# Differential attention's queries and keys projected feature by token, their rotation fed by DMA block exchanges

## The reference, cut to what matters

```python
def project(h):
    q, k, v, z = jnp.split(h @ w_in, 4, axis=-1)          # each 1024 wide: 8 heads x 2 x 64
    return (q.reshape(B, L, H, 2, d) * scale, k.reshape(B, L, H, 2, d),
            v.reshape(B, L, H, 2 * d), z)
def apply_axial_rope(t, cos, sin):                        # 64 features = 2 axes x 2 halves x 16
    tf = t.reshape(t.shape[:-1] + (2, 2, quarter))
    t1, t2 = tf[..., 0, :], tf[..., 1, :]
    return stack([t1 * c - t2 * s, t2 * c + t1 * s], axis=-2).reshape(t.shape)
q_l = apply_axial_rope(q_l, cos, sin)
k_l = apply_axial_rope(k_l, cos, sin)
k_all, v_all = concatenate([k_c, k_l], 1), concatenate([v_c, v_l], 1)
```

## Time and profile before

| | |
|---|---|
| median of 3 runs | 2618.03 us (2617.14 to 2624.84) |
| profiled execution, its own time | 2614.49 us |
| its span in the trace | 2612.7 us |
| stage of the change, first matmul to last result | 1573.37 to 2028.5 us of the span |
| TensorE busy | 89% of the span |

### The profile page before, as it was taken

How to read it: one execution, slowest core, us unless ns; L and a number is a source line. 1 busy time by engine, 2 the same in 40 slices (tenths; PEclk the granted TensorE clock), 3 DMA queues, 4 the chain that set the end, 5 groups by cost and what they waited for, 6 DMA issues and landing times. The chain is left out here.

```text
span 2612.7 us, 31980 instructions
## 1 busy us (share of the span) xinstructions
PE 2334.5 (89%) x12468; PEld 1926.5 (74%) x12468; DVE 1148.3 (44%) x2048; ACT 968.7 (37%) x1876; POOL 871.8 (33%) x713
## 2 busy tenths in 40 slices
PE   5999476998999999999999968998999699999596
PEld 4899334886888888888888847787788588888265
DVE  4455365771522222222225354544110588888233
ACT  5434343781512112211224242211121477777330
POOL 3432152453323122312231142111120477777330
PEclk8999677999999999999999989999999899999798
DMA  4265733632112011201111004333441535432411
GB/s 130 79 165 138 221 119 76 180 81 81 45 53 65 29 48 54 65 25 49 57 56 50 17 17 129 109 105 105 129 143 53 161 89 131 124 99 76 166 44 73
DMA packets 223511, 237.27 MB, mean 91 GB/s; under 512 B 63576, under 2 KB 158312, under 8 KB 223360
## 3 DMA queue, kind: packets, MB, share of 16 engines
q1 hardware_dynamic: 155520, 195.36, 25.7%
q10 hardware_dynamic: 67840, 39.86, 5.5%
HBM read 170.06 MB, written 65.10 MB: 90 GB/s over the span
## 5 line engine op out<-in xcount | busy, mean ns | idle before, releaser
L1860 POOL TENSOR_TENSOR rm_w_lo<-rm_stage,rm_w_hi 128x512 fp32r<-128x512 f32 x160 | 204.8, 1296 | 553.0 <-ACT rm_w_hi L1887 552.5
L1887 ACT ACTIVATE rm_w_hi<-rm_stage 128x512 fp32r<-128x512 f32 x160 | 97.6, 625 | 286.4 <-PE rm_down L326 233.2
L326 PE MATMUL rm_down<-rm_w_hi,rm_h_hi 128*128 128x512 f32 x512 | 203.1, 397 | 0.0
L2574 DVE TENSOR_REDUCE da_low_score<-da_scores 128x1 f32<-128x1280 f32 x128 | 190.2, 1487 | 28.8 <-PE da_scores L2456 28.7
L326 PE MATMUL rm_down<-rm_w_lo,rm_h_hi 128*128 128x512 f32 x512 | 202.5, 395 | 0.0
L326 PE MATMUL rm_down<-rm_w_hi,rm_h_lo 128*128 128x512 f32 x512 | 202.4, 395 | 0.0
L308 POOL TENSOR_TENSOR dp_w_lo<-dp_stage,dp_w_hi 128x512 fp32r<-128x512 f32 x64 | 82.2, 1288 | 333.4 <-ACT dp_w_hi L297 333.3
L2557 POOL TENSOR_TENSOR da_prob<-da_prob 128x1280 f32<-128x1280 f32 x64 | 188.4, 2943 | 5.3
L2015 DVE TENSOR_TENSOR residual<-residual,rm_down 128x512 f32<-128x512 f32 x128 | 87.5, 687 | 224.2 <-PE rm_down L326 223.6
L2456 PE MATMUL da_scores<-da_k_hi,da_q 128*128 128x512 f32 (+1 forms) x384 | 151.3, 394 | 30.7 <-DMA da_k_lo<-dk_lo 26.8
L2515 ACT ACTIVATE da_prob<-da_scores,da_low_score 128x1280 f32<-128x1280 f32 x128 | 170.3, 1331 | 7.4 <-DVE da_low_score L2574 7.3
(11 more groups left out here) (378 smaller groups left out, 6488.7 us busy)
## 6 DMA issues: line engine op xcount, KB each, us to landing
rm_stage<-in_w_mlp_up SPq DMA_DIRECT2D x64, 256.0 KB, 2.9
rm_stage<-in_w_mlp_down SPq DMA_DIRECT2D x64, 256.0 KB, 3.0
dp_stage<-in_da_w_in SPq DMA_DIRECT2D x64, 256.0 KB, 3.2
gla_ada_w<-in_ada_w SPq DMA_DIRECT2D x12, 1024.0 KB, 5.2
da_k_hi<-dk_hi SPq DMA_DIRECT2D x32, 320.0 KB, 9.7
da_k_lo<-dk_lo SPq DMA_DIRECT2D x32, 320.0 KB, 11.2
dq<-dp_out_hi ACTq DMA_DIRECT2D x32, 256.0 KB, 3.7
da_q<-dq SPq DMA_DIRECT2D x16, 512.0 KB, 8.4
```

What stands on the lines that cost most here:

```text
L326: last = nc.tensor.matmul(out, x, y, start=(n == 0), stop=(n == total - 1))
L1860: nc.gpsimd.tensor_tensor(lo, stage[:, n % SLOTS], hi.bitcast(F32), ALU.subtract).then_inc(w_lo_ready, 1)
L1887: nc.scalar.activation(hi, stage[:, n % SLOTS], ACT.Copy).then_inc(w_hi_ready, 1)
L2574: nc.vector.tensor_reduce(out=low_score[:, n, z:z + 1], in_=scores[z][:, 0:K], op=ALU.min, axis=AX.X).then_inc(low_score_ready, 1)
```

## The change

Queries and keys are now made feature by token, as z was: the weights are the stationary operand, the tokens the moving one. An output is (group, kind, f, half): 128 features x 512 tokens, and for K also one of 256 context columns for each f. There are 16 Q, 16 + 8 K, 20 V and 16 Z outputs, 76 in all; 32 of them ("rope" outputs) are rotated. Eight banks hold products and no bank is kept for transposes.

For the rotation ScalarE copies the product to `x`; SP issues 8 DMAs that exchange neighbouring blocks of 16 partitions into `swapped` (SBUF to SBUF); VectorE multiplies the product by a cosine table, the exchanged copy by a signed sine table, and adds. The tables (128 x 512 each) now depend on the token half and are reloaded when the half changes (4 times after the first). ScalarE and VectorE then make high and low part. All loads and stores are issued by SP in one written order; `out_hi` and `out_lo` have two buffers each. Attention loads the query by two DMAs instead of one.

```diff
--- before.py
+++ after.py
-        banks = c.banks("dp_ps", ctx, BANKS)
-        turn = [ctx.enter_context(nc.psum_tensor(f"dp_turn{i}", [P, 2 * NCOL], F32)) for i in range(2)]
+        table = sb("table", [P, 2, NCOL])
+        x, swapped = sb("x", [P, 2, NCOL]), sb("swapped", [P, 2, NCOL])
+        out_hi, out_lo = sb("out_hi", [P, 2, NCOL]), sb("out_lo", [P, 2, NCOL])
+        banks = c.banks("dp_ps", ctx)
...
+        def stored_before(engine, n):
+            if n >= 2:
+                engine.wait_ge(stored[n % 2], 16 * sum(1 + has_low[m] for m in range(n % 2, n, 2)))
         @block.sync
         def _(sp):
-            sp.dma_start(cos[:], a["da_cos"].rearrange("(t p) n -> p t n", p=P)).then_inc(loaded, 16)
-            sp.dma_start(sin[:], a["da_sin"].rearrange("(t p) n -> p t n", p=P)).then_inc(loaded, 16)
-            w.load(sp)
+            def load_table(r):
+                cols = slice(halves[r] * NCOL, (halves[r] + 1) * NCOL)
+                if r:
+                    sp.wait_ge(roped, r)
+                for i, name in enumerate(("da_cos", "da_sin")):
+                    sp.dma_start(table[:, i], a[name][:, cols]).then_inc(table_loaded, 16)
+            def swap(n):
+                r = rope_index[n]
+                sp.wait_ge(copied, r + 1)
+                if r >= 2:
+                    sp.wait_ge(roped, r - 1)
+                for at in range(0, P, 32):
+                    for u, v in ((at, at + 16), (at + 16, at)):
+                        sp.dma_start(swapped[u:u + 16, r % 2], x[v:v + 16, r % 2]).then_inc(swap_loaded[r % 2], 16)
+            def store(n):
...
+                for part, t in enumerate((out_hi, out_lo)[:1 + has_low[n]]):
+                    sp.wait_ge(*((lo_ready, lows_upto[n]) if part else (hi_ready, n + 1)))
...
+            for m in range(KT + 2):
+                w.load_chunk(sp, m)
+                if m == 2:
+                    load_table(0)
+            for n in range(N):
+                g = outs[n][0]
+                m = w.first[g + 1] + n - first_of[g] + 2
+                if n - first_of[g] < KT and m < G * KT:
+                    w.load_chunk(sp, m)
+                if n in rope_index:
+                    if rope_index[n] in changes:
+                        load_table(rope_index[n])
+                    swap(n)
+                if n >= 1:
+                    store(n - 1)
+            store(N - 1)
...
         @block.tensor
-            def turns(n):
...
+            for n, (g, kind, f, at) in enumerate(outs):
+                if n >= 8:
+                    m = n - 8
+                    if m in rope_index:
+                        pe.wait_ge(product_ready, rope_index[m] + 1)
...
         @block.scalar
+            def copy(n):
+                r = rope_index[n]
+                act.wait_ge(result_ready, n + 1)
+                if r >= 2:
+                    act.wait_ge(lo_ready, lows_upto[ropes[r - 2]])
+                nc.scalar.activation(x[:, r % 2], banks[n % 8][:], ACT.Copy).then_inc(copied, 1)
+            def high(n):
+                g, kind, f, at = outs[n]
+                if n in rope_index:
+                    act.wait_ge(roped, rope_index[n] + 1)
+                else:
+                    act.wait_ge(result_ready, n + 1)
+                stored_before(act, n)
...
+                if g + 1 < G and o < KT:
+                    w.split_hi(act, w.first[g + 1] + o)
+                if kind == "rope":
+                    copy(n)
+                if n - 1 in rope_index:
+                    high(n - 1)
+                if kind != "rope":
+                    high(n)
         @block.vector
+            def rotate(n):
+                r = rope_index[n]
+                i = r % 2
+                dve.wait_ge(table_loaded, 32 * (1 + sum(y <= r for y in changes)))
+                dve.wait_ge(swap_loaded[i], 16 * 8 * (r // 2 + 1))
+                nc.vector.tensor_tensor(x[:, i], banks[n % 8][:], table[:, 0], ALU.mult).then_inc(product_ready, 1)
+                nc.vector.tensor_tensor(swapped[:, i], swapped[:, i], table[:, 1], ALU.mult).then_inc(sine_ready, 1)
+                dve.wait_ge(product_ready, r + 1)
+                dve.wait_ge(sine_ready, r + 1)
+                nc.vector.tensor_tensor(x[:, i], x[:, i], swapped[:, i], ALU.add).then_inc(roped, 1)
...
+            for n in range(N):
+                if n in rope_index:
+                    rotate(n)
+                if n - 1 in rope_index:
+                    low(n - 1)
+                if n not in rope_index and has_low[n]:
+                    low(n)
 def differential_attention:
-                for place, src in ((q[:, s, z], d["dq"][h, z]), (k_hi[0:DD, s, z], hi), (k_hi[DD:P, s, z], hi),
+                rows = slice(z * DD, (z + 1) * DD)
+                for place, src in ((q[0:DD, s, z], d["dq"][h, 0, rows]), (q[DD:P, s, z], d["dq"][h, 1, rows]),
+                                   (k_hi[0:DD, s, z], hi), (k_hi[DD:P, s, z], hi),
```

More of the change, by code:

```diff
@@ L2162, in differential_project, with places_of @@
     G = 8
+    FT = NCOL // P
+    Q_SCALE = -DD ** -0.5
     groups = [[WIN[k * P:(k + 1) * P, g * NCOL:(g + 1) * NCOL] for k in range(KT)] for g in range(G)]
[L2164 to L2170, removed]
+    def places_of(g):
+        if g in V_G:
+            return [("values", None, t) for t in range(TT + CT)]
+        kind = "z" if g in Z_G else "rope"
+        out = [(kind, f, h) for h in ((0, 1) if g % 2 == 0 else (1, 0)) for f in range(FT)]
+        return out + ([("context", f, None) for f in range(FT)] if g in K_G else [])
+    outs = [(g,) + x for g in range(G) for x in places_of(g)]
+    N = len(outs)
+    done_at = [sum(x[0] <= g for x in outs) for g in range(G)]
+    first_of = [sum(x[0] < g for x in outs) for g in range(G)]
+    ropes = [n for n in range(N) if outs[n][1] == "rope"]
+    rope_index = {n: r for r, n in enumerate(ropes)}
+    halves = [outs[n][3] for n in ropes]
+    changes = [r for r in range(1, len(ropes)) if halves[r] != halves[r - 1]]
+    has_low = [x[1] != "z" for x in outs]
+    lows_upto = [sum(has_low[:n + 1]) for n in range(N)]
+    parts_upto = [n + 1 + lows_upto[n] for n in range(N)]
     with ExitStack() as ctx:
@@ L2191, in _, with columns, width @@
+        def columns(n):
+            _, kind, f, at = outs[n]
+            return slice(S, S + CTX) if kind == "context" else slice(at * NCOL, (at + 1) * NCOL)
+        def width(n):
+            return CTX if outs[n][1] == "context" else NCOL
+        def stored_before(engine, n):
+            if n >= 2:
+                engine.wait_ge(stored[n % 2], 16 * sum(1 + has_low[m] for m in range(n % 2, n, 2)))
         @block.sync
         def _(sp):
-            sp.dma_start(cos[:], a["da_cos"].rearrange("(t p) n -> p t n", p=P)).then_inc(loaded, 16)
@@ new lines, in store @@
+            def store(n):
+                g, kind, f, at = outs[n]
+                i = n % 2
+                for part, t in enumerate((out_hi, out_lo)[:1 + has_low[n]]):
+                    sp.wait_ge(*((lo_ready, lows_upto[n]) if part else (hi_ready, n + 1)))
+                    h = 4 * (g % 2) + (f or 0)
+                    if g in Q_G:
+                        place = d["dq"][h, part, :, columns(n)]
+                    elif g in K_G:
+                        place = d[("dk_hi", "dk_lo")[part]][h].rearrange("z p s -> (z p) s")[:, columns(n)]
+                    elif g in V_G:
+                        place = d[("dv_hi", "dv_lo")[part]][h:h + 4, :, at, :].rearrange("h p n -> p h n")
+                    else:
+                        place = d["dz"][h, :, columns(n)]
+                    held = t[:, i, 0:width(n)]
+                    sp.dma_start(place, held.rearrange("p (h n) -> p h n", h=4) if g in V_G else held)\
+                        .then_inc(stored[i], 16)
@@ L2197, in _ @@
+            store(N - 1)
+            for i in range(2):
+                sp.wait_ge(stored[i], 16 * sum(1 + has_low[m] for m in range(i, N, 2)))
         @block.gpsimd
@@ L2230, in _ @@
[L2230 to L2250, removed]
+                    if kind == "values":
+                        xs, t = ((c.Xhi, c.Xlo), at) if at < TT else ((ctx_hi, ctx_lo), at - TT)
+                        terms.append((tuple(y[:, k, t * P:(t + 1) * P] for y in xs), ww))
+                    else:
+                        xs = ((ctx_hi, ctx_lo) if kind == "context" else (c.Xhi, c.Xlo))
+                        cols = slice(0, CTX) if kind == "context" else columns(n)
+                        terms.append((tuple(y[:, f * P:(f + 1) * P] for y in ww), tuple(y[:, k, cols] for y in xs)))
@@ L2252, in _, with source @@
+                product(nc, banks[n % 8][:, 0:width(n)], terms, width(n), result_ready,
+                        (lambda k: pe.wait_ge(w.lo_ready, w.first[g] + k + 1)) if n == first_of[g] else None)
+        def source(n):
+            return x[:, rope_index[n] % 2] if n in rope_index else banks[n % 8][:, 0:width(n)]
         @block.scalar
         def _(act):
```

(5 more changed lines are left out.)

100 lines of the change are left out of this document (22 added, 78 removed).

## The result

The changed kernel takes 2677.41 us (median of 4 runs, 2672.45 to 2680.12); the kernel before took 2617.59 beside it (4 runs, 2613.98 to 2624.84). The ratio is 1.0226, interval 1.0202 to 1.025: slower by 59.8 us, where 29 were forecast. The time lay inside the stated range of 2612 to 2695.

A forecast was written before the change was run, and what follows sets the result against it. TensorE bound the old stage; a closed exchange loop would bound the new one. Stage end +28.5 and attention's load +0.5 gave +29 on 2614.5, 2643.5; the median, 3.5 higher, 2647. Range 2612 to 2695.

The forecast's parts named there:

- The ring: Rope outputs: closed loop of copy, exchanges, rotation and low part, no two exchanges overlapping; period 9.05 us against TensorE's 5.44.
- s: Distance between SP's exchange issues: 0.475 us, read from back-to-back weight loads; bounds 0.38 and about 0.6.
- W: Exchange time per rope output, 7s + L: 5.33 us, bounds 4.36 and 7.3; stage end = 1907.8 + 28W.
- The rest of the ring: Rope output's period beside W: low part, low store, chunk load and VectorE's operations, carried as 3.72 us.
- L: Time from an output's last exchange issue to its landing: 2.0 us, bounds 1.7 and 3.1.
- The cheap rival: Exchanges cheap, s 0.33 and L 1.5: W 3.8, stage ends 14 us earlier than before, median 2604; chance 0.08.
- The dear rival: Exchanges dear, issues at 0.6 and landing at 3.0: W 7.2, +84 us, 2702; chance 0.14.
- The end of the stage: Predicted at 2057.0, +28.5 us; V's fourth output 17.2 after rope output 30's exchange, then 33 outputs in 179.5.
- The clock and the idle time: TensorE idles 3.6 us per rope period and may drop to 1.2 GHz; only one slow start counted before V.
- The rival in which it stays slow: TensorE at the lower clock through all of Q and K, 43 outputs x 10.25: about 2784; chance 0.01.
- The rival without a ring: No closed loop, TensorE the bound, transposes and rotation waits saved: -28 us, 2590; chance 0.01.
- Attention's start: Six DMAs instead of five ahead of attention's first scores: one more issue, +0.5 us.

The follow-up runs named there:

- e1: Changed kernel with three buffers for x instead of two, SP's order kept: 2674.05 us, ratio 1.0235 to the kernel before.
- e2: Changed kernel with VectorE making the low part of output n-1 before it rotates n: 2590.3 us, ratio 0.992 to the kernel before.
- e7: Changed kernel with SP issuing the stores of output n-2 instead of n-1, two buffers for x: 2663.67 us, ratio 1.0185 to the kernel before.
- e8: Changed kernel with SP issuing the stores of n-2 and three buffers for x: 2593.28 us, ratio 0.9919 to the kernel before.
- e3: Changed kernel with exchanges replaced by plain copies or DRAM loads of eight forms, to read issue distances: 2633.24 us (one run).
- e6: Changed kernel with the edits of e2 and e5 together: 2558.62 us, ratio 0.9788 to the kernel before.
- e5: Changed kernel with four of the eight exchanges issued by ScalarE, ring kept: 2621.63 us, ratio 1.0037 to the kernel before.

## Why the forecast was right in direction and half in size

**The ring, right.** VectorE waits 32 times for an exchange, ScalarE's copy for the low part, SP for the low store, and no second exchange is issued before the first is used. e1, e2, e7 and e8 show that the ring holds the period, and that the two reasons named in the forecast (x's two buffers and SP's order) are both in force; the forecast had not said that curing one of them is worth nothing.

**The term that failed: s.** The forecast took 0.475 us between issues, "since these exchanges are plain rows issued back to back". Measured: 0.62. Seven distances make 7 x 0.145 = 1.0 us a period, and W 6.34 instead of 5.33. e3 shows what the 0.475 did not carry over to: loads from DRAM are 0.46 apart even over 16 partitions, copies within SBUF 0.63 in each of the three other forms of eight shown. The upper bound at 0.59 was the nearest row in value and was passed over for its 64 partitions. By the forecast's own formula 28 x 1.01 = 28 us are to be added to the end of the stage, and it came 29.7 later: this one term is nearly all of the miss. What makes such an issue cost 0.62 stays open.

**What else moved.** The rest of the ring was 3.67, not 3.72: 27 x 0.05 = 1.4 us less. The low store took 0.33 of it where 0.53 was forecast, and gaps took most of that back. The start came 2.8 earlier, which says little: the stage's first matmul starts anywhere from 1567 to 1574 us in the profiles of the nine kernels with the new code, and at 1573.4 in the kernel before. Against it, single periods were longer, with 10.7 to 11.2 us four times before rope output 23, the table changes not counted. In one of them a chunk's issue took 1.24 us on SP where 0.43 is the rule; in the other three the eight exchanges took 5.6 to 6.1 to issue. These outliers make 227.6 - 22 x 10.01 - 3 x 1.0 = 4.4 us, which the forecast had at nothing.

**L, right.** 2.0 forecast, 2.0 measured. By the Trainium skill (SBUF - State Buffer, "Door 1: The DMA port swizzle") the estimate for 16 partitions was 2.3. The trace doesn't show that: the 32 KB exchanges land in a median of 2.0. The cheap rival fell by s and L both. The dear rival had s right (0.6) and L wrong (3.0); the truth took s from it and L from the forecast.

**The end of the stage, right in number and partly by luck.** From the exchange of rope output 30 to V's fourth output it took 17.14 us (17.2 forecast), but not on the path forecast. The last weight chunk let TensorE go on at 1891.95 with three matmuls of V's first output left. Seven matmuls ran at the lower clock where the forecast had 16, so V's third output was through at 1905.2, only 15.5 us after the exchange. Then TensorE waited 1.68 us for VectorE to free the bank of the last rope output (the row at 1906.90 above), a wait that the forecast had said doesn't decide. That bank comes one period, one W and one multiplication after the exchange of output 30 (10.0 + 6.4 + 0.7), so it was late by the mis-sized s as well, and this hid that the forecast's path was 1.7 too long. The 33 outputs took 179.8 (179.5 forecast), and V and Z kept 5.44.

**The clock and the idle time, right in kind.** The forecast had TensorE idle for 3.6 us in each period. It ran ahead instead and waited in bulk: 12 waits of 5.5 to 9.4 us make up nearly all of its idle time after the start of the stage. After each of them it started at the lower level, 1.2 GHz: matmuls of 512 columns 0.43 apart as in the earlier trace rows, and of 256 columns 0.21 apart.

```profile
1891.95 0.79 PE L326 MATMUL dp_ps<-dp_w_hi,xb_hi 128*128 128x512 f32 x1 [7.92 <-POOL dp_w_lo L308]
1892.54 0.63 PE L326 MATMUL dp_ps<-dp_w_lo,xb_hi 128*128 128x512 f32 x1
1892.97 0.63 PE L326 MATMUL dp_ps<-dp_w_hi,xb_lo 128*128 128x512 f32 x1
```

It came back to full speed within the output or the next (0.87 in the window). At V's fourth output TensorE had 1.68 us to spare in spite of it, so there the slow matmuls cost nothing; that they cost nothing elsewhere follows only from the ring setting the pace. The rival in which it stays slow did not occur.

**The rival without a ring, right in kind, too small.** It was put at 28 us below before; e6 is such a kernel, 55 below. It priced a 256-column matmul at one weight load, 0.178 us, where 0.12 was measured (192 x 0.058 = 11 us), and counted only the 8 us of rotation waits where idle time and slow clock together gave 26.

**Attention's start.** +0.5 forecast for one more issue, +2.0 measured; one pair of loads there took 2.14 us to issue where 1.24 is usual. It took 1.65 to 2.28 in each of the other kernels with the new code too, and 1.15 in the kernel before, so with the one issue more (0.6) about 1.5 of the 2.0 are accounted for. Why this pair is slow is open.

## What to carry over

When an output passes through copy, DMA and rotation on three in-order engines, write down which instruction each one stands behind and look for a ring before you count buffers: a spare buffer is worth nothing while a queue's order holds the same edge, and swapping two statements was worth 82 to 84 us. Price many small DMAs by issues on one engine, with a row of the same kind (here SBUF to SBUF cost 0.62 where the weights' loads from DRAM cost 0.475), and read such rows from a microtest when the trace has none. Once the ring was open the bound moved to the issuing queue, and a second issuing engine took that away too. And when a stretch comes out at the forecast number, look at which wait ended last in it before you call it right.

## What was not expected of the hardware

- Issues of SBUF-to-SBUF DMAs behind each other on one queue start 0.61 to 0.63 us apart, for 16, 32, 64 or 128 partitions and for 4 to 64 KB. 16-partition loads from DRAM start 0.46 apart. A store takes 0.58 to issue behind the one, 0.43 behind the other, 0.33 alone. Attention's loads from DRAM over 64 partitions start 0.64 apart (two take 1.24), so the source alone isn't the rule; what the rule is stays open.
- 256 KB from SBUF to SBUF in one DMA land in 3.6 us, the last of eight of 32 KB in 2.0 us.
- With two engines issuing at a time (e5) the landing grew from 2.0 to 2.5 us, the issue distance stayed.
- Matmuls of 256 columns run 0.12 us apart in e6, below the 0.19 us that each of their weight loads is busy in the profile: that busy time is not what sets their pace.
